# Two narrow products in four column groups, sums of squares added on VectorE, and the scan's inputs prepared beside z

## The reference, cut to what matters

```python
def rmsnorm(x, g, eps):            # the root mean square over 1024 features
    return x * rsqrt(mean(x * x, -1) + eps) * g

# mixer of layer 0 (mixer_even)
proj = h @ w_in
a_val, a_gate, z, xbc, dt_raw = split(proj)      # 512, 512, 512, 1024, 8 columns
a_conv = causal_dwconv(a_val * sigmoid(a_gate), conf_state, conf_w, conf_b)  # 31 taps
a_out = silu(layernorm(a_conv, ln_g, ln_b))      # mean and variance over 512 features
xbc_c = silu(causal_dwconv(xbc, ssd_conv_state, xbc_w, xbc_b))               # 4 taps
xs, b_in, c_out = split(xbc_c)
dt = softplus(dt_raw + dt_bias); a = -exp(a_log)
cs = cumsum(dt * a) in each 128-frame chunk
y, new_state = ssd_scan(xs, dt, a, b_in, c_out, ssd_state)
b_out = rmsnorm((y + d_skip * xs) * silu(z))
out = concatenate([a_out, b_out]) @ w_out

# mixer of layer 1 (mixer_odd): eight of its 3080 columns are the forget gate
logf = log_sigmoid(f_raw + f_bias); f_cum = cumsum(logf)
```

## Time and profile before

| | |
|---|---|
| median of 3 runs | 1990.05 us |
| lowest, highest | 1987.34 us, 1992.46 us |
| profiled execution, its own time | 1988.97 us |
| profiled execution, its span | 1986.8 us |
| TensorE busy (matmuls) | 1891.7 us, 95% of the span |
| VectorE busy | 733.3 us, 37% |
| ScalarE busy | 451.0 us, 23% |
| GpSimd busy | 142.2 us, 7% |

### The profile page before, as it was taken

How to read it: one execution, slowest core, us unless ns; L and a number is a source line. 1 busy time by engine, 2 the same in 40 slices (tenths; PEclk the granted TensorE clock), 3 DMA queues, 4 the chain that set the end, 5 groups by cost and what they waited for, 6 DMA issues and landing times.

```text
span 1986.8 us, 26525 instructions
## 1 busy us (share of the span) xinstructions
PE 1891.7 (95%) x11410; PEld 1589.4 (80%) x11410; DVE 733.3 (37%) x1179; ACT 451.0 (23%) x718; POOL 142.2 (7%) x149
## 2 busy tenths in 40 slices
PE   7999988999989999999989998999998999999998
PEld 5755557555589999999969997655567999999998
DVE  2089954323343222232341303522245323223322
ACT  3200142114232111112231123411333211111211
POOL 3001100010000000000032323100000000000000
PEclk9999988999999999999999999999999999999999
DMA  6322130150222123121212252502312211222120
GB/s 229 127 72 68 44 127 6 43 233 22 75 74 66 62 73 105 64 78 44 80 64 64 84 65 88 184 23 100 133 44 85 69 65 59 94 84 84 44 93 33
DMA packets 32035, 161.50 MB, mean 81 GB/s; under 512 B 8584, under 2 KB 9224, under 8 KB 18016
## 3 DMA queue, kind: packets, MB, share of 16 engines
q1 hardware_dynamic: 24032, 121.97, 18.9%
q0 software_dynamic: 7936, 38.60, 5.3%
HBM read 149.87 MB, written 10.42 MB: 81 GB/s over the span
## 4 chain that ended last, share of the span: by engine, by line
PE 92%; DVE 4%; ACT 2%; issue 1%; DMA 0%; POOL 0%; ACTq 0%; DVEq 0%
PE G L630 85%; PE Q L630 3%; PE S L630 2%; ACT rstd L1173 1%; DVE front L1508 1%; PE Q L1106 1%; DVE work L1813 1%; DVE h_split L1817 1%; ACT work L1173 0%; ACT front L1173 0%; PE Q L961 0%; DVE stats L1940 0%; DMA front<-in_mem 0%; DVE front L1953 0%; DVE stats L1751 0%
## 5 line engine op out<-in xcount | busy, mean ns | idle before, releaser
L630 PE MATMUL G<-h_split,w_split 128*128 128x320 f32 x5184 | 768.3, 310 | 10.9 <-DVE h_split L1817 10.8
L630 PEld LDWEIGHTS G<-h_split,w_split 128*128 128x128 f32 x5184 | 764.1, 189 | 13.1 <-issue 8.9
L630 PE MATMUL G<-front,ring 128*128 128x512 f32 (+2 forms) x1792 | 485.8, 432 | 10.6 <-DVE front L1508 7.0
L630 PEld LDWEIGHTS G<-front,ring 128*128 128x128 f32 x1792 | 278.2, 192 | 217.6 <-issue 211.8
L630 PE MATMUL G<-g_split,w_split 128*128 128x320 f32 x2112 | 310.4, 309 | 0.0
L630 PEld LDWEIGHTS G<-g_split,w_split 128*128 128x128 f32 x2112 | 309.9, 188 | 0.0
L1544 DVE TENSOR_TENSOR w_split<-ring,w_split 128x1024 fp32r<-128x1024 f32 (+2 forms) x152 | 164.5, 1083 | 359.4 <-ACT w_split L1173 359.4
L1173 ACT ACTIVATE w_split<-ring 128x1024 fp32r<-128x1024 f32 (+2 forms) x172 | 164.4, 958 | 517.7 <-PE G L630 517.7
L1173 ACT ACTIVATE work<-G 128x640 f32<-128x640 f32 x52 | 36.7, 706 | 331.9 <-PE G L630 331.9
L1594 DVE SCALAR_TENSOR_TENSOR front<-front,par 128x512 f32<-128x512 f32 x240 | 111.6, 546 | 0.1
L1829 DVE TENSOR_TENSOR work<-work,G 128x640 f32<-128x640 f32 x44 | 36.2, 822 | 183.8 <-PE G L630 183.8
(11 more groups left out here) (213 smaller groups left out, 1068.8 us busy)
## 6 DMA issues: line engine op xcount, KB each, us to landing
ring<-in_w_up0a SPq DMA_DIRECT2D x11, 1024.0 KB, 4.8
ring<-in_w_up0b SPq DMA_DIRECT2D x11, 1024.0 KB, 4.8
ring<-in_w_up1a SPq DMA_DIRECT2D x11, 1024.0 KB, 4.8
ring<-in_w_up1b SPq DMA_DIRECT2D x11, 1024.0 KB, 4.9
front<-in_mem_k POOLq DMA_DIRECT2D x8, 1024.0 KB, 13.0
front<-in_mem_v POOLq DMA_DIRECT2D x8, 1024.0 KB, 14.9
ring<-in_w_down0a SPq DMA_DIRECT2D x8, 704.0 KB, 4.0
ring<-in_w_down0b SPq DMA_DIRECT2D x8, 704.0 KB, 4.1
```

Source lines behind the costliest of these rows:

```text
L630: return nc.tensor.matmul(out, lhsT, rhs, start=start, stop=stop, **kw)
```

## The change

The step sizes and the forget gate (`narrow`) are computed in four groups of 32 output columns: slice `k` of `h` goes to column group `k % 4`, so that the four groups hold four partial sums on partitions 0, 32, 64 and 96. ScalarE copies them to SBUF, and one more product with a matrix of zeros and ones (`narrow_sum`) adds the four. The step sizes come right behind `glu`, with `narrow_sum` after the first `xbc` tile; the forget gate's `narrow_sum` comes after the five `fv` tiles. The squares of `x` for the first norm, and the slices for the convolution's mean and variance, are added on VectorE, and TensorE sums over partitions once. The softplus and cumulative sums of the step sizes (lines 1635 to 1660, now the function `decay_sums`) move ahead of slice 4 of the `xbc` convolution, and `tok` ahead of `z` 2 and 3. The convolution's instructions are divided 32, 32, 32, 10 and 142 instead of 36, 36, 36 and 140. The load of the scan's states is issued earlier. The memory products of both layers stay in front of `glu`.

```diff
@@ TensorE @@
-            def narrow(name, wname, normed=None):
-                out = begin(TILE0[name])
+            def narrow(n, wname, normed=None):
+                out = begin(n)
                 pe.wait_ge(par_in, 16)
-                o = PAR[wname][0]
                 for k in range(KD):
                     if normed is not None:
                         pe.wait_ge(applied, normed + k)
-                    w = par[:, o + k * NH:o + (k + 1) * NH]
-                    mm(out[0:NH, 0:512], w, h[:, k, 0:512], k == 0, k == KD - 1)
-                    m = mm(out[0:NH, 512:T], w, h[:, k, 512:T], k == 0, k == KD - 1)
+                    q, o = k % 4, PAR[wname][0] + k * NH
+                    rows, w = slice(32 * q, 32 * q + 32), par[:, o:o + 32]
+                    mm(out[rows, 0:512], w, h[:, k, 0:512], k < 4, k >= 4, tile_position=(0, 32 * q))
+                    m = mm(out[rows, 512:T], w, h[:, k, 512:T], k < 4, k >= 4, tile_position=(0, 32 * q))
                 m.then_inc(tile_done, 1)
+
+            def narrow_sum(n, n_parts, parts):
+                out = begin(n)
+                read_wait(pe, n_parts)
+                pe.wait_ge(const_in, 16)
+                mm(out[0:NH, 0:512], cst("d8"), parts[:, 0:512], True, True)
+                mm(out[0:NH, 512:T], cst("d8"), parts[:, 512:T], True, True).then_inc(tile_done, 1)
...
                     if l == 0 and n == 1:
-                        for k in range(KD):
-                            stat(k, KD, ones)
+                        residual_stat(0)
...
             projections("glu", 8, KD, rows(h), norm="mix0")
-            projections("xbc", 8, KD, rows(h))
-            narrow("dt", "wdt")
-            pe.wait_ge(conv, 8 * CW)
-            for k in range(4):
-                stat(k, 4, ones, src=acc[:, k, :])
-            projections("z", 4, KD, rows(h), after=lambda n: n == 2 and [stat(k, 4, ones) for k in range(4)])
+            narrow(TILE0["dtp"], "wdt")
+            for n in range(8):
+                if n % 2 == 0:
+                    s = chunk(CHUNK["xbc"] + n // 2)
+                project(xbc_tile(n), s, n % 2 * P, KD, rows(h))
+                if n == 0:
+                    narrow_sum(TILE0["dt"], TILE0["dtp"], dt_parts)
+            conv_stat(3)
+            s = chunk(CHUNK["z"])
+            for n in range(2):
+                project(z_tile(n), s, n % 2 * P, KD, rows(h))
+            nready[0] += 4
+            conv_stat(6)
...
+            s = chunk(CHUNK["z"] + 1)
+            for n in range(2, 4):
+                project(z_tile(n), s, n % 2 * P, KD, rows(h), halfway=h_free if n == 3 else None)
...
-            narrow("f", "wf", APPLIED["mix1"] - KD + 1)
+            narrow(TILE0["fp"], "wf", APPLIED["mix1"] - KD + 1)
             sa, sc = chunk(CHUNK["fv"]), chunk(CHUNK["fv"] + 1)
             for c in range(NCH):
                 frame_major(TILE0["fv"] + c, lambda k: h[:, k, c * P:(c + 1) * P], sa, sc)
+            narrow_sum(TILE0["f"], TILE0["fp"], f_parts)
@@ VectorE @@
+            for j in range(KD):
+                add_square("x", j)
             norm_x("mix0")
...
-                conv_taps(36 if j < 3 else 8 * CW - 3 * 36)
+                conv_taps(32 if j < 3 else 10)
+            step_sizes()
+            conv_taps(8 * CW - taps_done[0])
+            def conv_sum(first, ready, part):
...
+                for k in range(1, 4):
+                    ready(k)
+                    if k > 1:
+                        dve.wait_ge(conv_added, first + k - 1)
+                    v.tensor_tensor(total, part(0) if k == 1 else total, part(k), ALU.add).then_inc(conv_added, 1)
+            conv_sum(0, lambda k: dve.wait_ge(conv, 8 * CW), lambda k: acc[:, k, :])
...
             for j in range(KD):
+                if j == 3:
+                    subtract_mean()
                 if j == 4:
-                    step_sizes()
-                    subtract_mean()
+                    decay_sums()
+                    conv_sum(3, lambda k: dve.wait_ge(sq_ready, 24 + k + 1), lambda k: sq[:, k % 2, :])
@@ ScalarE, from the last glu tile on @@
+            evacuate(dt_parts, TILE0["dtp"])
+            log_exp_table()
...
+            xbc_rows(0)
+            act.wait_ge(dt_abs, 1)
+            own(A(dtb[:, 2, :], dtb[:, 2, :], ACT.Exp, scale=-1.0))
...
+            for j in range(1, 8):
+                xbc_rows(j)
+            for j in range(2):
+                xbc_silu(j)
...
+            xbc_silu(2)
             act.wait_ge(applied, APPLIED["mean"])
             for k in range(4):
-                square(acc[:, k, :])
+                if k < 2:
+                    square(acc[:, k, :])
+                else:
+                    act.wait_ge(conv_added, 3 + 1)
+                    A(sq[:, nsq[0] % 2, :], acc[:, k, :], ACT.Square).then_inc(sq_ready, 1)
+                    nsq[0] += 1
+            xbc_silu(3)
+            z_gate(0)
+            xbc_silu(4)
+            z_gate(1)
+            xbc_silu(5)
             log_exp_table()
             act.wait_ge(cs_ready, 1)
             A(dtb[:, 2, :], dtb[:, 2, :], ACT.Exp, scale=-1.0).then_inc(de_ready, 1)
+            inv_std(1, 1.0 / CONF, eps=1)
...
+            for j in range(6, KD):
+                xbc_silu(j)
+            z_gate(2)
+            act.wait_ge(h_free, 1)
             for k in range(4):
+                act.wait_ge(applied, APPLIED["var"] - 3 + k)
                 A(h[:, k, :], acc[:, k, :], ACT.Silu, scale=pr("lng", k), bias=pr("lnb", k)).then_inc(mixed, 1)
+            z_gate(3)
             log_exp_table()
@@ GpSimd @@
             for j in range(KD):
+                if j == 6:
+                    pool.wait_ge(early_outs, 16 * EARLY_OUTS)
+                    pool.wait_ge(conv, 8 * CW)
+                    pool.wait_ge(xbc_done, 1)
+                    pool.dma_start(h0T, dram["ssd_state"]).then_inc(state_in, 16)
...
             stores_landed()
-            pool.wait_ge(xbc_done, KD)
-            pool.dma_start(h0T, dram["ssd_state"]).then_inc(state_in, 16)
```

More of the change, by code:

```diff
@@ L74 @@
                ("xq0", 1), ("xq1", 1), ("xk0", 1), ("xk1", 1), ("dskip", 4),
-               ("dtb", 1), ("alog", 1), ("fb", 1), ("wdt", KD * NH), ("wf", KD * NH)):
+               ("dtb", 1), ("alog", 1), ("fb", 1)):
     _place(PAR, _n, _w)
 TILE = {}
-for _n, _c in (("mk0", 4), ("mv0", 2), ("mk1", 4), ("mv1", 2), ("glu", 8), ("xbc", 8), ("dt", 1), ("z", 4),
-               ("tok", 2), ("evout", 8),
+for _n, _c in (("mk0", 4), ("mv0", 2), ("mk1", 4), ("mv1", 2), ("glu", 8), ("dtp", 1), ("xbca", 1), ("dt", 1), ("xbc", 7),
+               ("za", 2), ("tok", 1), ("zb", 2), ("evout", 8),
                ("q0", 4), ("xo0", 10), ("xt0", 2), ("wo0", 8), ("up0a", KH), ("down0a", 8), ("up0b", KH), ("down0b", 8),
-               ("f", 1), ("fv", NCH), ("cgu", 8), ("gb", 4), ("fqk", 8),
+               ("fp", 1), ("fv", NCH), ("f", 1), ("cgu", 8), ("gb", 4), ("fqk", 8),
                ("odout", 8),
@@ L152, with xbc_tile, z_tile @@
 _cross_ffn("1")
+def xbc_tile(j):
+    return TILE0["xbc"] + j - 1 if j else TILE0["xbca"]
+def z_tile(j):
+    return TILE0["z" + "ab"[j // 2]] + j % 2
 FQK = [0, 4, 1, 5, 2, 6, 3, 7]
@@ L297, in build @@
         fl = r(T, rows=NH)
-        fx = r(T, rows=NH)
+        f_parts = r(T)
+        fx = f_parts[0:NH]
         fcp = mv[0:NH, 0, 0, :]
@@ L488, in _, with store @@
             stores = [0]
-            def store(dst, src):
-                pool.dma_start(dst, src).then_inc(outs, 16)
-                stores[0] += 1
+            def store(dst, src, early=False):
+                pool.dma_start(dst, src).then_inc(early_outs if early else outs, 16)
+                stores[0] += not early
             def stores_landed():
@@ L654, in project @@
                         m = mm(out[:, 512:width], w, rhs(k)[:, 512:width], first, last)
+                    if halfway is not None and k == KT // 2 - 1:
+                        m.then_inc(halfway, 1)
                 m.then_inc(tile_done, 1)
@@ L1264, in _, with memory @@
                 act.wait_ge(x_in[k // 2], 16)
-                square(x[:, k, :])
-            residual_inv_std(KD)
-            for l in range(LAYERS):
+                residual_square(0, None, k)
+            residual_inv_std(2)
+            def memory(l):
                 head_norms(lambda j: mkT[:, l, j, :], TILE0[f"mk{l}"], 4, 1.0 / P, MT)
@@ L1642, in _ @@
-            own(v.tensor_scalar(dtb[:, 0, :], dtb[:, 1, :], small[0:NH, 3:4], -1.0, ALU.mult, ALU.mult))
-            segments = [(c * P, P) for c in range(4)] + [(SEQ + q * STEP, STEP) for q in range(REQ)]
-            one = cst("ones", NH)[:, 0:1]
-            for at, w in segments:
-                ins = v.tensor_tensor_scan(out=dtb[:, 3, at:at + w], data0=one.broadcast_to([NH, w]), data1=dtb[:, 0, at:at + w],
-                                           initial=0.0, op0=ALU.mult, op1=ALU.add)
```

208 lines of the change are left out of this document (111 added, 97 removed).

## The result

| | before | after |
|---|---|---|
| median | 1990.05 us | 1997.33 us (7 runs, 1995.16 to 1997.72) |
| profiled execution, own time | 1988.97 us | 1996.55 us |
| its span | 1986.8 us | 1994.8 us |

The ratio of after to before is 1.0035, with a 95% interval of 1.0023 to 1.0046: the change costs 0.2 to 0.5%. That is inside the predicted range (1986 to 2001), on the slow side of the forecast (1994.4). By the prediction's own line of 6 us between same and slower, the measured 7 us lie on the slower side of the line, but the line is inside the interval (4.6 to 9.2 us).

What follows compares the result with a forecast made beforehand. TensorE, busy 95% of the span, was taken as the bound, so edits count by shortening its work or making it wait. 0 + 3.2 (14.0 - 10.8) + 1.1 = +4.3 us on 1990.05 gave 1994.4, range 1986 to 2001.

Steps and rivals of the forecast that it cites:

- the squares of x: Before `glu`: six matmuls fewer but TensorE waits for VectorE's adds; between 2.1 us gain and 1.8 loss, taken as 0.
- `glu` to the scan: From `glu` to the scan's start: VectorE's late chain and the clock make the scan start 14.0 us later.
- what the scan gives back: In the scan: a shorter gap and a higher clock return 10.8 us; 8.5 if the clock stays low, 14.5 if never.
- forget gate: Forget gate's product: paced by VectorE's norm, so packing saves nothing and `narrow_sum` adds 1.1 us.
- VectorE's lateness: Convolution to `tok`: VectorE idles ahead of `step_sizes`, so TensorE waits 9.1, 7 to 9 and 7 to 9 us.
- The four groups: Step sizes' `narrow`: 2.3 us instead of 8.8, priced by cross attention's request steps (32 records in 1.86 us).
- rival (1): In `narrow`: the groups don't overlap, it takes 7.9 us and `dt` comes 5.6 later; 2000.0 us, chance 0.12.
- The clock in `z`: The two `z` tiles behind `tok`: low clock after the waits costs up to 3.7 us, taken as 2.5.
- the gap: Between `scan_ahead(0)` and `scan_ahead(1)`: 8.2 us becomes some 3.2, since silus and a table load move under `z` 3.
- Later chunks are the same: In the scan: the chunks after the 92 records were to take as long as before.
- rival (3): The clock pays less: front gains 2.1, `z` loses 0, scan returns 14.5; 1985.2 to 1984.1 us, chance 0.14.
- rival (2): The clock pays more: front +1.8, `z` 3.7, scan returns only 8.5; +9.6 in all, 1999.7 us, chance 0.24.

Runs made afterwards that it cites:

- Experiment 1: The changed kernel with its convolution taps divided 36, 36, 36 and 26 ahead of the step sizes instead of 32, 32, 32 and 10: 1984.59 us, ratio 0.9978.
- Experiment 4: The changed kernel with useless 512-frame matmuls (10, 9 and 9) filling TensorE's three waits: 1994.91 us, ratio 1.0028.
- 6: The changed kernel with the forget gate as before: one group, no second product, VectorE's part ahead of the `fv` tiles: 1995.10 us, ratio 1.0035.
- experiment 5: The changed kernel with the squares of x summed by eight TensorE matmuls again, without adds on VectorE: 1997.10 us, ratio 1.0051.
- experiments 1 to 6: Includes one run without its own line: the changed kernel with the step sizes' product in one group of eight columns again, 2000.76 us, ratio 1.0062.
- experiment 3: The kernel before with only the step sizes' four-group product and its sum added, at the old place behind `xbc`: 1985.18 us, ratio 0.9987.

## Why the prediction was right

The sum was to be +4.3 us, the profiles have +7.6, the ratio gives 7.0 (4.6 to 9.2). The working's steps against the profile after:

| step | predicted | measured |
|---|---|---|
| the squares of x, at the start of `glu` | 0 | +1.4 |
| `glu` to the scan | +14.0 | +13.7 |
| what the scan gives back | -10.8 | -9.2 |
| forget gate | +1.1 | +1.4 |

The rows add up to 7.3, and the span grew by 8.0; the other 0.7 lie in stages that the working took as unchanged. So the time came out right with two terms off by 1.4 and 1.6 us, both the same way, which the range covered. By the prediction's own chances this was not the likelier side: it gave "slower" than +6 us 0.38 and "same" 0.54.

**VectorE's lateness**, the heart of the argument, came as worked out: idle 6.64 us ahead of `step_sizes` (6.4 by the sum), TensorE's waits 9.09, 6.83 and 7.38 (9.1; 7 to 9, missed by 0.2; 7 to 9), the scan at 299.8 of which 1.4 is from the front (298.7). Experiment 1 shows it as the cause: with the taps divided otherwise the first wait vanishes, and 10.9 us between `glu` and the scan with it. Experiment 4 shows that the low clock behind the waits is some 2 us of the price, and not what makes the waits.

**The four groups** took 2.40 us for the 2.3 chosen by the attention row, and rival (1) fell: in one group the same product takes 8.78 and the kernel 3.4 us more (5.4 by the ratios). By the Trainium skill's rule on program order ("TensorE: Matmul & The Clock Gate", Part 3) the four groups would have taken 7.9, by the prediction's estimate; the row of 2.40 disagrees.

**The clock in `z`** was put at 2.5, beside `tok` at half clock. Experiment 4 measures `tok`, the two tiles and ScalarE's part: 297.58 - 278.00 = 19.6 at full clock against 21.8, so 2.2, of which the tiles have 1.5 (19.06 against 17.57). In the profiles of experiments 1 and 6 the same tiles took 20.05 and 20.53, so the term is between 1.5 and 3.0 from profile to profile.

**The scan** gave 4.9 back in the gap (5.0 predicted), 2.4 in `scan_ahead(1)` (2.3), 3.7 in the 92 records (3.5). "Later chunks are the same" failed: the second stretch of low clock lay, by the profile's clock records, from 313.5 to 327.2, where before it was from 305.6 to 319.2, and took in all of `scan_ahead(2)` and most of the next 36 records (5.39 us for 4.04). That lost 1.8, the largest step that was mis-sized. The bounds of this term don't follow from its parts either: 5.0, 2.3 and 6.0 make 13.3, and no row is given for the rest of the 14.5; and a clock that stays low would leave 5.0, not 8.5. So rival (3) is 1.2 us too low and rival (2), under its own condition, 3.5 too low; neither touches the forecast.

**The squares of x.** The chosen 0 fits what the runs can tell: experiment 5 takes the edit back and finds neither time nor an earlier `glu`, and with the edit `glu` starts as early as 87.21. The 1.4 in the table goes with the clock under which each execution passes the first tiles: the profile before is the only one of the eight compared below that keeps 1.00 from 20 to 45 us. That this is chance and not the edit is likely by these starts, and not shown for the medians.

**The forget gate.** 1.1 and 1.4 agree. The cover for VectorE's part held: it ends at 1090.4, and `cgu` comes at 1097.07.

Rival (2), that the clock pays more, came in part, and the time lies half way to it. Its three terms would have had the front at +1.8, `z` at 3.7 and the scan at -8.5. The profile after has +1.4, which no run shows to be the edit's; 1.5 to 2.2 in `z`, nearer to the forecast; and -9.2 in the scan, nearer to the rival.

## What to carry to other kernels

When two engines hand work to and fro in fixed orders, look for the one that never pauses in the trace, and count what a new order makes it wait for: here 12 us of slack on VectorE was spent by putting a short step, which waits for TensorE, ahead of 142 of its instructions, and moving 28 of them in front of that step was worth more (10.9 us up to the scan) than all the packing (6.3). Work to fill an engine's waits should be chosen by what else it drags along: the values' product needed only buffers and an order on ScalarE, the keys' product needed GpSimd. After each move look for the instruction that now waits and read what stands queued behind it.

## What the runs showed of the hardware that was not expected

**GpSimd can be held off for tens of microseconds by VectorE.** Two GpSimd instructions of 0.7 and 0.5 us took 22.20 and 28.07 beside VectorE's runs of instructions that read two SBUF tensors, and ended when those runs ended. With the same scaling on VectorE the kernel was 45 us faster.

**The start of the program has more than one course.** With the same instructions, or nearly so, `glu` started between 87.2 and 89.3 us in eight profiles (before, after, and experiments 1 to 6), and the granted clock from 20 to 45 us was 0.80 to 1.00. The windows of the kernel before, of experiment 3, and of the kernel after:

```profile
20.00:45.00 25.00, 21.68 (x91) 15.87 (x90) 7.60 (x10) 12.38 (x24) 12.10 (x16) 1.00 0.62 160
```

```profile
20.00:45.00 25.00, 21.68 (x83) 15.54 (x83) 7.29 (x9) 11.83 (x23) 11.18 (x13) 0.93 0.57 136
```

```profile
20.00:45.00 25.00, 16.84 (x58) 12.35 (x57) 12.09 (x15) 11.70 (x23) 10.86 (x13) 0.86 0.57 137
```

The first two run the same instructions there and are busy for the same 21.68 us, but at 0.93 TensorE got through 83 records and at 1.00 through 91. Of 23 runs of the kernel before in one set, each lies near one of five values, 1985.3, 1987.3 to 1988.2, 1989.1 to 1990.3, 1992.5 to 1992.7 and 1995.0 to 1995.3. That these steps of some 2.5 us come from where the clock's low stretches fall is argued, not shown. It is why one profile beside another can't settle a difference of 2 us here.
